# A first gate and up product without the root of the norm, and initial loads in turns

## The reference, cut to what matters

```python
def rms_norm(x, w):
    xf = x.astype(jnp.float32)
    y = xf * lax.rsqrt(jnp.mean(xf * xf, axis=-1, keepdims=True) + EPS)
    return (y * w.astype(jnp.float32)).astype(x.dtype)

def swiglu(x, w_gate, w_up, w_down):
    return (jax.nn.silu(x @ w_gate) * (x @ w_up)) @ w_down

x = x + 0.5 * swiglu(rms_norm(x, ffn1_norm[l]), ffn1_w_gate[l], ffn1_w_up[l], ffn1_w_down[l])
```

## Time and profile before

| what | value |
|---|---|
| median of three runs | 2685.14 us |
| the profiled execution's own time | 2686.26 us |
| its span | 2684.4 us |
| mean granted TensorE clock | 0.989 of full speed |
| PE busy | 2594.5 us, 97% of the span |
| DVE, ACT busy | 1679.0 us, 1094.6 us |
| DMA | 380.98 MB, mean 142 GB/s |

### The profile page before, as it was taken

The page is one execution under the profiler, slowest core; times in us unless marked ns, Lnnn a source line. Parts: engine busy times, 40 slices in busy tenths (PEclk is TensorE's granted clock), DMA queues, the critical chain, the costliest instruction groups (busy, mean ns, idle before and its releaser), DMA issues.

```text
span 2684.4 us, 38719 instructions
## 1 busy us (share of the span) xinstructions
PE 2594.5 (97%) x15836; PEld 2299.7 (86%) x15836; DVE 1679.0 (63%) x2665; ACT 1094.6 (41%) x1707; POOL 64.1 (2%) x60
## 2 busy tenths in 40 slices
PE   7999898999999999999999999999999999998998
PEld 7998797999888888778888888889888888888998
DVE  6767545777677555666545767665555456776654
ACT  5446654555322224343244332224232234655543
POOL 0001030000000000000100000000000000000000
PEclk9999999999999999999999999999999999999999
DMA  7764202675555442112222455543443433244454
GB/s 262 236 231 174 88 9 72 212 237 174 167 187 190 158 143 94 51 40 87 93 89 94 149 180 185 176 159 111 146 133 130 141 110 103 74 142 161 161 181 146
DMA packets 110113, 380.98 MB, mean 142 GB/s; under 512 B 12016, under 2 KB 17392, under 8 KB 109552
## 3 DMA queue, kind: packets, MB, share of 16 engines
q1 hardware_dynamic: 108928, 373.32, 41.9%
q10 hardware_dynamic: 1008, 5.18, 0.5%
HBM read 377.40 MB, written 1.05 MB: 141 GB/s over the span
## 4 chain that ended last, share of the span: by engine, by line
PE 89%; DVE 5%; ACT 3%; issue 2%; DMA 0%; SPq 0%; ACTq 0%; DVEq 0%
PE B L1464 26%; PE B L1466 25%; PE B L1465 25%; ACT w_hi L1785 2%; DVE w_lo L2085 2%; PE B L1724 1%; PE B L1707 1%; PE B L1479 1%; PE B L1618 1%; PE B L1480 1%; PE B L1481 1%; PE B L1631 1%; PE B L1714 1%; DVE AC L2330 1%; DVE TMP L2112 0%
## 5 line engine op out<-in xcount | busy, mean ns | idle before, releaser
L1464 PE MATMUL B<-U,w_hi 128*128 128x256 f32 (+1 forms) x2896 | 961.7, 332 | 8.1 <-DVE w_lo L2085 8.0
L1465 PE MATMUL B<-U,w_hi 128*128 128x256 f32 (+1 forms) x2896 | 952.3, 329 | 0.0
L1466 PE MATMUL B<-U,w_lo 128*128 128x256 f32 (+1 forms) x2896 | 952.1, 329 | 0.0
L2085 DVE TENSOR_TENSOR w_lo<-w_raw,w_hi 128x1024 fp32r<-128x1024 f32 (+3 forms) x587 | 685.4, 1180 | 408.8 <-ACT w_hi L1785 407.7
L1785 ACT ACTIVATE w_hi<-w_raw 128x1024 fp32r<-128x1024 f32 (+3 forms) x587 | 590.8, 1012 | 505.3 <-PE B L1466 482.6
L1464 PEld LDWEIGHTS B<-U,w_hi 128*128 128x128 f32 x2896 | 546.1, 189 | 64.6 <-issue 8.1
L1465 PEld LDWEIGHTS B<-U,w_hi 128*128 128x128 f32 x2896 | 547.0, 189 | 53.7 <-issue 2.2
L1466 PEld LDWEIGHTS B<-U,w_lo 128*128 128x128 f32 x2896 | 545.6, 188 | 51.7
L1464 PE MATMUL B<-HHf,w_hi 128*128 128x256 f32 (+1 forms) x1122 | 364.6, 325 | 1.6 <-DVE w_lo L2085 1.6
L1466 PE MATMUL B<-HHf,w_lo 128*128 128x256 f32 (+1 forms) x1122 | 363.8, 324 | 0.0
L1465 PE MATMUL B<-HLf,w_hi 128*128 128x256 f32 (+1 forms) x1122 | 363.8, 324 | 0.0
(11 more groups left out here) (353 smaller groups left out, 2585.0 us busy)
## 6 DMA issues: line engine op xcount, KB each, us to landing
w_raw<-in_w SPq DMA_DIRECT2D x504, 512.0 KB, 4.2
w_ada<-in_w SPq DMA_DIRECT2D x144, 512.0 KB, 3.4
w_raw<-in_w SPq DMA_DIRECT2D x58, 384.0 KB, 3.2
w_raw<-in_w SPq DMA_DIRECT2D x16, 240.0 KB, 2.5
X<-in_x SPq DMA_DIRECT2D x2, 1024.0 KB, 9.7
w_raw<-in_w SPq DMA_DIRECT2D x8, 256.0 KB, 2.8
BW<-in_bias ACTq DMA_DIRECT2D x1, 1536.0 KB, 10.4
K<-in_consts ACTq DMA_DIRECT2D x2, 640.0 KB, 5.5
```

The source lines that it names most:

```text
L1464: pe.matmul(o, hi, xh, start=i == 0 and s.start, stop=False)
L1465: pe.matmul(o, hi, xl, start=False, stop=False)
L1466: e = pe.matmul(o, lo, xh, start=False, stop=i == last and s.stop)
L2085: dve.tensor_tensor(w_lo[:, plan.slot[u], 0:n], w_raw[:, plan.ring[u], 0:n], w_hi[:, plan.slot[u], 0:n].bitcast(F32), ALU.subtract).then_i ...
```

## The change

It does four things.

1. A new function `begin_raw` takes the place of the first norm and the first pair. A step `raw` multiplies a chunk of X by the norm's weight alone, rounds it on ACT into a region UO of U that is free at this point, and takes the remainder on DVE. The pairs j=0 and j=1 are computed from UO, in halves of four chunks, and the sum over the partitions for the root stands between the two halves of j=1.
2. Since the banks of j=0 and j=1 lack the root, a step `ffn_raw` multiplies it in: gate bank by root (DVE), Silu (ACT), times the up bank (DVE), times the root again (DVE), rounded (ACT), remainder (DVE). It replaces `ffn_h` for these two tiles. The tiles from j=2 on use the normalized U as before.
3. X is loaded in two halves, the 8 columns of the norm's weight apart from the other columns, and weights in between.
4. `fetch` steps can say how far ahead they split (`arg`), and the `ahead` step inside the norm stands after chunk 2, where it stood after chunk 5.

```diff
@@ with_splits
-                while done < min(at + AHEAD + 1, len(cut)) and (done < NH or cut[done - NH] in used):
+                ahead = s.arg if s.kind == "fetch" and s.arg is not None else AHEAD
+                while done < min(at + ahead + 1, len(cut)) and (done < NH or cut[done - NH] in used):
@@ norm_to_u
-            if k == 5:
+            if k == ahead:
                 self.add("ahead")
@@ ffn
+            if j < raw:
+                self.add("ffn_raw", key=(p, j), n=n, b=g, b2=u, t=t, need=old, rb=rb)
+                self.PS.done(g, ("gr", (p, j)))
+                self.PS.done(u, ("ur", (p, j)))
...
+            else:
+                self.add("ffn_h", key=(p, j), n=n, b=g, b2=u, t=t, need=old)
@@ Plan
+    def begin_raw(self):
+        wts = [self.weights([("f1" + x, k, 128 * j, 128) for k in range(8) for x in "gu"]) for j in range(2)]
+        banks = [(self.PS.get(), self.PS.get()) for _ in range(2)]
...
+        def half(j, k0):
+            self.add("pair", key=keys[j] if k0 else (), wts=wts[j][2 * k0:2 * k0 + 8], x="UO", n=256, b=banks[j][0], b2=banks[j][1],
+                     k0=k0, need=need)
+
+        for k in range(4):
+            self.add("raw", key=("raw", k), n=256, x="UO")
+        self.add("fetch", u=wts[0][0][0], arg=0)
+        for k in range(4, 8):
+            self.add("raw", key=("raw", k), n=256, x="UO")
+        self.add("fetch", u=wts[0][8][0], arg=0)
+        stat = Stat(self, "x", 256)
+        for k in range(8):
+            stat.add_("X", k, ("x", k // 4))
+            if k == 3:
+                self.add("fetch", u=wts[0][8][0], arg=1)
+        half(0, 0)
+        half(0, 4)
+        half(1, 0)
+        rb = stat.rsqrt(D)
+        self.norm_to_u("ffn1_norm", rb, None, 2)
+        half(1, 4)
+        return {k: b for ks, bs in zip(keys, banks) for k, b in zip(ks, bs)}, rb
@@ whole
-        stat = Stat(self, "x", 256)
-        for k in range(8):
-            stat.add_("X", k, ("x", 0))
-        wts = self.fetch(self.first_of("f1"))
-        rb = stat.rsqrt(D)
-        need = self.norm_to_u("ffn1_norm", rb, None)
+        begun, rb = self.begin_raw()
         self.add("cs")
-        keys = [("f1", "g", 0), ("f1", "u", 0)]
-        stat = self.ffn("f1", 256, dict(zip(keys, self.pair(keys, wts, 256, need))), None, ())
+        stat = self.ffn("f1", 256, begun, None, (), raw=2, rb=rb)
@@ scalar
+            elif k == "raw":
+                act.activation(HI[s.x][:, c, :], X[:, c, 0:256], ACT.Copy,
+                               scale=col("ffn1_norm", c)).then_inc(*up("uh", s.key))
+            elif k == "ffn_raw":
+                w.wait_ge(*at("gr", s.key))
+                act.activation(TM(s.t, s.n), TM(s.t, s.n), ACT.Silu).then_inc(*up("silu", s.key))
+                w.wait_ge(*at("hm", s.key))
+                w.each(s.need)
+                act.activation(HI[p][:, j, :], TM(s.t, s.n), ACT.Copy).then_inc(*up("hh", s.key))
@@ vector
+            elif k == "raw":
+                dve.scalar_tensor_tensor(
+                    out=LO[s.x][:, c, :], in0=X[:, c, 0:256], scalar=col("ffn1_norm", c), in1=HI[s.x][:, c, :].bitcast(F32),
+                    op0=ALU.mult, op1=ALU.subtract).then_inc(*up("ul", s.key))
+            elif k == "ffn_raw":
+                dve.tensor_tensor(h, PS(s.b, s.n), r, ALU.mult).then_inc(*up("gr", s.key))
+                w.wait_ge(*at("silu", s.key))
+                w.wait_ge(*at("mm", (p, "u", j)))
+                dve.tensor_tensor(h, h, PS(s.b2, s.n), ALU.mult).then_inc(*up("ur", s.key))
+                w.wait_ge(*at("ur", s.key))
+                dve.tensor_tensor(h, h, r, ALU.mult).then_inc(*up("hm", s.key))
+                w.wait_ge(*at("hh", s.key))
+                dve.tensor_tensor(LO[p][:, j, :], h, HI[p][:, j, :].bitcast(F32), ALU.subtract).then_inc(*up("hl", s.key))
@@ sync
-        sp.dma_start(X[:, :, 0:256], xs[:, :, 0:256]).then_inc(*landed("x", 0))
-        sp.dma_start(PC[:, 0:ncol], cols).then_inc(*landed("cols", 0))
-        sp.dma_start(C1[:], consts[:, 0:256]).then_inc(*landed("c1", 0))
-        for u in plan.cut[:NR]:
-            sp.dma_start(w_raw[:, plan.ring[u], 0:plan.units[u][1]], source(u)).then_inc(*landed(f"w{plan.ring[u]}", u))
+        sp.dma_start(X[:, 0:4, 0:256], xs[:, 0:4, 0:256]).then_inc(*landed("x", 0))
+        sp.dma_start(PC[:, 0:8], cols[:, 0:8]).then_inc(*landed("gain1", 0))
+        weights(plan.cut[0])
+        sp.dma_start(X[:, 4:8, 0:256], xs[:, 4:8, 0:256]).then_inc(*landed("x", 1))
+        weights(plan.cut[1])
+        sp.dma_start(C1[:], consts[:, 0:256]).then_inc(*landed("c1", 0))
+        for u in plan.cut[2:NR]:
+            weights(u)
+        sp.dma_start(PC[:, 8:ncol], cols[:, 8:ncol]).then_inc(*landed("cols", 0))
```

More of the change, by code:

```diff
@@ L365, in ada, with norm_to_u @@
                 self.add("derive", key=(l, b // 24))
-    def norm_to_u(self, name, rb, wait_u):
+    def norm_to_u(self, name, rb, wait_u, ahead=5):
         late = None
@@ L380, in norm_to_u @@
         self.TM.done(late, ("ul", (name, 7)))
-        self.RB.done(rb, ("nt", (name, 7)))
+        if not ahead < 5:
+            self.RB.done(rb, ("nt", (name, 7)))
         return tuple(("ul", (name, k)) for k in range(8))
@@ L411, in down, with ffn @@
         return [(p + "d", k, 128 * m, 128) for k in range(NF)]
-    def ffn(self, p, n, begun, gate, old, stat=None, beside=None):
+    def ffn(self, p, n, begun, gate, old, stat=None, beside=None, raw=0, rb=None):
         turns, share = 0, lambda i: min(i * ADA[p] // ADAS[p], ADA[p])
@@ L417, in ffn @@
         for j in range(NF):
-            g, u = (begun.get((p, x, j)) or self.gemm((p, x, j), [(p + x, k, 128 * j, 128) for k in range(8)], n)
+            need = tuple(("ul", ("ffn1_norm", k)) for k in range(8)) if raw and j == raw else ()
+            g, u = (begun.get((p, x, j)) or self.gemm((p, x, j), [(p + x, k, 128 * j, 128) for k in range(8)], n, need=need)
                     for x in "gu")
             t = self.TM.get()
-            self.add("ffn_h", key=(p, j), n=n, b=g, b2=u, t=t, need=old)
-            self.PS.done(g, ("silu", (p, j)))
-            self.PS.done(u, ("hm", (p, j)))
+            if j < raw:
+                self.add("ffn_raw", key=(p, j), n=n, b=g, b2=u, t=t, need=old, rb=rb)
+                self.PS.done(g, ("gr", (p, j)))
+                self.PS.done(u, ("ur", (p, j)))
+                if j == raw - 1:
+                    self.RB.done(rb, ("nt", ("ffn1_norm", 7)), ("hm", (p, j)))
+            else:
+                self.add("ffn_h", key=(p, j), n=n, b=g, b2=u, t=t, need=old)
+                self.PS.done(g, ("silu", (p, j)))
+                self.PS.done(u, ("hm", (p, j)))
             self.TM.done(t, ("hl", (p, j)))
@@ L441, in ffn @@
         return stat
+    def begin_raw(self):
+        wts = [self.weights([("f1" + x, k, 128 * j, 128) for k in range(8) for x in "gu"]) for j in range(2)]
+        banks = [(self.PS.get(), self.PS.get()) for _ in range(2)]
+        keys = [[("f1", x, j) for x in "gu"] for j in range(2)]
+        need = tuple(("ul", ("raw", k)) for k in range(8))
+        def half(j, k0):
[19 more added lines that the diff above has]
+        return {k: b for ks, bs in zip(keys, banks) for k, b in zip(ks, bs)}, rb
     def whole(self):
         self.add("load")
-        stat = Stat(self, "x", 256)
-        for k in range(8):
-            stat.add_("X", k, ("x", 0))
-        wts = self.fetch(self.first_of("f1"))
-        rb = stat.rsqrt(D)
-        need = self.norm_to_u("ffn1_norm", rb, None)
+        begun, rb = self.begin_raw()
         self.add("cs")
-        keys = [("f1", "g", 0), ("f1", "u", 0)]
-        stat = self.ffn("f1", 256, dict(zip(keys, self.pair(keys, wts, 256, need))), None, ())
+        stat = self.ffn("f1", 256, begun, None, (), raw=2, rb=rb)
         wts = self.fetch([("win", k, 128 * j, 128) for k in range(8) for j in range(2)])
@@ L1765, in scalar @@
                 table = "exp"
-            elif k in ("ffn_h", "conv_silu", "gate_silu", "ln_out", "glu_g", "bgate", "cs"):
+            elif k in ("ffn_h", "ffn_raw", "conv_silu", "gate_silu", "ln_out", "glu_g", "bgate", "cs"):
                 table = "other"
```

13 lines of the change are left out of this document (added).

## The result

The changed kernel takes 2699.2 us (median of 4 runs, 2696.84 to 2704.57), beside 2685.66 us of the kernel before (4 runs, 2680.0 to 2686.89). The ratio is 1.0058 with a 95% interval of 1.0033 to 1.0083: slower. The profiled execution took 2704.57 us, 18.3 more than that of before (2686.26).

A forecast was written before the change was run, and what follows sets the result against it. PE, busy 97% of the span, was taken as the bound, with gains only in its waits before 15.75 us. A later j=3 (8.8) plus low clock (2.4) made 11.2 us on 2685.14, so 2696.3 us, range 2690 to 2701.

The forecast's parts named there:

- first product: Kernel start: PE's first matmul at 9.5 instead of 15.75, after unit 0 lands at 6.9 and is split.
- unit 4 landed: SP's load queue: unit 4 still lands at 22.65, bounds 22.0 to 23.6, and the root waits for it.
- unit 6's split starts: ACT, behind the Silu of CS and two raw tiles taking 4.3 us: starts at 40.6.
- first matmul of j=3: PE, after unit 6's split and remainder: 43.0 instead of 34.17, +8.8 us.
- lost to the low clock: PE behind the idle stretch before j=3: low clock costs 2.4 us, bounds 0 to 2.6.
- The chain: ACT and DVE from unit 4's landing at 22.65 through norm, Silu of CS and raw tiles to j=3 at 43.0.
- the last wait: PE ahead of j=3: idle 4 us, from j=2's end at 39.0 to 43.0.
- the sum: Whole kernel: 8.8 + 2.4 = 11.2 us slower, 2696.3 us; terms together from +7.5 to +13.
- (a): Rival, kernel start: PE's head start survives, 4.8 us faster, 2680.3 us; chance 0.05.
- (b): Rival, root not held by the DMA: j=3 at 40.2, +6.0, 2693.5 us with the clock, 2691.1 without; chance 0.12.
- (c): Rival, wait before j=3 as forecast but clock stays high: 8.8 us or less, 2693.9 us; chance 0.13.
- (d): Rival, second wait because tiles j=3 and j=4 can't catch up: 2 to 3 us more, 2699 us; chance 0.08.

The follow-up runs named there:

- e7: Changed kernel plus 46 filler matmuls, result unread, between j=2 and j=3 where PE waits; 2695.11 us, ratio 1.0041 to the kernel before.
- e0: The changed kernel measured once more, unaltered; 2696.97 us, ratio 1.0060 to the kernel before.
- e1: Changed kernel with CS, the second half of X and two w_ada loaded behind units 5, 6, 7; 2687.79 us, ratio 1.0033 to the kernel before.
- e4: Changed kernel with root and norm ahead of the splits of units 4 and 5; 2686.60 us, ratio 1.0014 to the kernel before.
- e3: Changed kernel with the Silu of CS moved behind the splits of units 6 and 7; 2691.44 us, ratio 1.0036 to the kernel before.
- e2: Changed kernel with j=2's products, and so the splits, listed ahead of CS's Silu and the raw tiles; 2692.51 us, ratio 1.0031 to the kernel before.
- e9: Kernel before, with PE made to wait ahead of six tiles in each of the first block's two feed-forward layers; 2718.46 us, ratio 1.0117.

## Why the prediction was right in its mechanism and low in its size

| step of the prediction | forecast | measured |
|---|---|---|
| first product | 9.5 | 8.66 |
| PE through with j=1 | 23.9 at the latest | 23.27 |
| unit 4 landed | 22.65 | 22.72 |
| first norm instruction | 24.9 | 24.97 |
| last rounding ends | 33.2 | 33.19 |
| first raw Silu | 36.3 | 36.33 |
| unit 6's split starts | 40.6 | 40.60 |
| first matmul of j=3 | 43.0 | 42.95 |
| lost to the low clock | 2.4 | 2.6, 2.0 (e7 beside e0) |
| behind by j=6 | 11.2 | 11.4, 11.7 (e0) |
| total by the medians | 11.2 | 13.5, 16.0 (e0) |

**The chain held to 0.1 us.** Every link was taken from rows of before in which the same instructions stood in another order, or, for the raw tiles, like ones. e1 and e4 show the head of the chain (the split that waits for the DMA, with the root behind it), e3 the Silu of CS as a link, and e2 that the wait ahead of j=3 is that of the raw tiles and CS in front of unit 6's split. That unit 4's landing was met to 0.1 us is luck in part, since the next execution had its split 0.8 us later.

**The first product** came 0.8 us sooner than forecast, and e0 shows why that is worth nothing: there it came at 10.07, and j=3 followed unit 4. The rows of before gave no landing for a unit that stands so far ahead in the queue; the two profiles have its split at 6.31 and 7.70.

**The shape of the waits** was a little off. I let j=2 end at 39.0 at the low clock. It ended at 37.51, so the last wait was 5.45 us and not 4. The sum doesn't hang on it, since the end of the wait was set by ACT and DVE.

**The step that failed** is the sum, whose last sentence is "The terms together run from +7.5 to +13": it took the start of the kernel for the only place where the time could change. (The bounds as listed there add up to +7.4 and +13.5.) The earlier trace rows gave 0.113 us per matmul, and I held that to be fixed at the high clock, so everything behind the start stood in the sum at nothing. But the spacing has two levels, which can change behind a wait, and each layer begins behind a wait in both kernels. In the profile of the changed kernel the second layer came out wide, for 5.7 us, and in e0's again; another 1.4 us came from a longer low clock at 1124. So the two profiled executions are 18.3 us apart where the start makes 11.4. For the profile of before the levels were to be seen: the last layer has 852 matmuls in 100 us where the others have 885, at the same granted clock, and I had not looked there. The missing term is 0 or about +6 us for each of the feed-forward layers, in both kernels. The 2.3 us by which the medians lie above the forecast (13.5 - 11.2), or 4.8 by e0 (16.0 - 11.2), are of a size with it, but the unprofiled runs don't show their spacing, so that share is argued and not shown.

**The rivals.** (a) fell: the head start is used up by 23.27, when PE waits for U. (b) fell: the root was held by the DMA in both profiles, and e1 is what it would have looked like (forecast 40.2 for j=3, measured 39.02, the root starting at 20.18 and not at 21.2). (c) fell for the changed kernel, whose clock was at 0.50 behind the wait; e7 shows what it would have been worth. (d) fell: after 42.95 no wait follows in the first 150 us.

**What stays open.** Is the wide spacing more frequent in the changed kernel, or was it chance? Two of two profiles had it in the second layer, the kernel before had not; of the seven runs of e0 two stand in the lowest group, of the 26 runs of before sixteen. That speaks for more frequent, but seven runs and two profiles don't settle it, and e1, e3 and e7 had the second layer narrow. Nor do I know what sets the level.

## What to carry to other kernels

When work is moved ahead on one engine, write down for every other engine what stands in its queue before the next instruction that somebody waits for: here a split that waited for a DMA stood in front of the root, and a head start of 7.1 us became a delay of 8.8, of which moving the load gives back 3.9 (e1) and moving the root 6.3 (e4); the two overlap, as each frees the root from the DMA. Follow the engines that feed PE to the point at which they have caught up, since work postponed from one tile's path can land in front of the next (e2; in e3 it didn't). Before a difference of less than 10 us is put down to an edit, compare the matmuls per 100 us in the stages that the edit doesn't touch.

## What the runs showed of the hardware

**Two spacings at one clock.** Matmuls of 128x256 follow each other at 0.1133 or 0.1178 us, both at a granted clock of 1.00 (885 or 851 in 100 us). A level often holds for 100 us and more, and may be another after the next wait (e9). It can also change without one: in the changed kernel from wide to narrow between 640.3 and 641.0, where the steps from start to start were 0.118, then 0.125, 0.114, 0.123, 0.118, and from there on 0.113 to 0.114. In the eleven other profiles ten of the 33 feed-forward layers on 256 columns were wide, in whole or for the most part. The matmuls on 512 columns had one spacing, 0.2267 us, in the long stretches of all of them.

**A wait's length alone doesn't tell the clock behind it.** PE came out of waits of 1.58 to 1.95 us at a granted clock of 1.00 at eleven of twelve places, and out of one of 2.05 us (e4). It was at 0.50 to 0.59 behind the waits of 2.52, 3.28 (e2), 5.45 and 5.8 us. In between it went both ways. The one other place of e9, a wait of 1.95 us ended at 574.67, was followed by 32 matmuls in 5 us at 0.66, while the other wait of 1.95 us (145.30) left the clock at 1.00. Behind the wait of 2.47 us that ended at 1124.05 in the changed kernel there were 8 matmuls in 5 us at 0.50; in e2 the same wait, ended at 1123.77, left the clock at 1.00:

```profile
1123.80:1128.80 5.00, 5.00 (x15) 1.00 0.00 0
```

Three microseconds each behind three of the waits of e9:

```profile
52.00:55.00 3.00, 3.00 (x26) 1.00 0.40 156
71.00:74.00 3.00, 3.00 (x26) 1.00 0.87 303
90.00:93.00 3.00, 3.00 (x28) 1.00 0.94 313
```

**A granted clock of 1.00 with half the matmuls.** From 9 to 14 us the changed kernel shows 25 matmuls in 5 us, as many as at 0.50 to 0.52 in the earlier trace rows, while the row says 1.00. Those 25 start 0.213 us apart, and the next ones 0.113. So I go by the count at this place and not by the column.

**The table load.** It took 1.28 us, and the next activation began 0.01 us after it (33.21 + 1.28 = 34.49, then 34.50). The Trainium skill (ScalarE: Activation LUTs, What ACT_TABLE_LOAD costs) adds a drain of about 1380 ns; the changed kernel shows none at this place either, and a chain with it would have brought j=3 to 44.3 instead of 42.95.
